# Modulation chunks of the first layer: three as rows on TensorE in the last head slots, one chunk step a head on VectorE, gate rows copied by ScalarE

## What is computed

```python
mod = (c_act @ ada_w[layer] + ada_b[layer])[:, None, :]
sh_a, sc_a, gt_a, sh_m, sc_m, gt_m = jnp.split(mod, 6, axis=-1)
h = modulate(rms_norm(x, attn_norm[layer]), sh_a, sc_a)
mix = diff_attention(h, a_w_in[i], a_w_out[i], a_lambda[i], a_subln[i], rel_bias, layer)
x = x + gt_a * mix
h = modulate(rms_norm(x, mlp_norm[layer]), sh_m, sc_m)
x = x + gt_m * squared_relu_mlp(h, mlp_w1[layer], mlp_w2[layer])
```

## Time and profile before

| what | us |
|---|---|
| median of 3 runs | 1377.74 |
| lowest, highest | 1368.96, 2510.94 |
| the profiled execution | 1370.68 |
| its span in the trace | 1368.9 |
| mean granted TensorE clock | 0.976 of 2.4 GHz |

### The profile page before, as it was taken

The page is one execution under the profiler, slowest core; times in us unless marked ns, Lnnn a source line. Parts: engine busy times, 40 slices in busy tenths (PEclk is TensorE's granted clock), DMA queues, the critical chain, the costliest instruction groups (busy, mean ns, idle before and its releaser), DMA issues.

```text
span 1368.9 us, 22008 instructions
## 1 busy us (share of the span) xinstructions
PE 1297.5 (95%) x8462; PEld 1125.1 (82%) x8462; DVE 883.9 (65%) x1593; ACT 682.8 (50%) x1196; POOL 139.0 (10%) x166
## 2 busy tenths in 40 slices
PE   7879899999989999989999988999999999999999
PEld 3678798998879865789999876799998777898987
DVE  3579789999676377785544676665655656644453
ACT  2546454435355346544545685554444566654442
POOL 0122111001000000010101121011010101011000
PEclk9989999999999799999999999999999999999999
DMA  9997449999787332286665252296565464466650
GB/s 350 344 290 230 159 136 341 331 332 332 250 246 197 119 124 94 64 289 208 183 192 166 91 184 63 93 272 225 178 189 171 138 194 140 134 194 186 186 166 32
DMA packets 144776, 267.42 MB, mean 195 GB/s; under 512 B 11040, under 2 KB 50208, under 8 KB 144288
## 3 DMA queue, kind: packets, MB, share of 16 engines
q1 hardware_dynamic: 138592, 250.94, 57.1%
q0 software_dynamic: 3456, 12.58, 2.8%
q10 hardware_dynamic: 2624, 2.49, 0.6%
HBM read 264.83 MB, written 1.15 MB: 194 GB/s over the span
## 4 chain that ended last, share of the span: by engine, by line
PE 67%; DVE 13%; DMA 7%; issue 6%; ACT 4%; SPq 1%; POOL 1%; DVEq 0%; ACTq 0%; POOLq 0%
PE bank L542 12%; PE bank L544 12%; PE bank L543 12%; DMA wring<-in_mlp_w 4%; PE ps_s L542 4%; PE ps_s L543 4%; PE ps_s L544 4%; PE ps_p L542 3%; PE ps_p L543 3%; PE ps_p L544 3%; DVE wlo L1585 3%; DVE acc L1604 3%; DMA xn<-in_ada_w 2%; ACT whi L2746 2%; DVE acc L1633 1%
## 5 line engine op out<-in xcount | busy, mean ns | idle before, releaser
L1585 DVE TENSOR_TENSOR wlo<-wring,whi 128x1024 fp32r<-128x1024 f32 (+1 forms) x376 | 455.0, 1220 | 298.4 <-ACT whi L2746 295.3
L2746 ACT ACTIVATE whi<-wring 128x1024 fp32r<-128x1024 f32 (+1 forms) x376 | 388.5, 1045 | 389.3 <-PE bank L544 143.2
L542 PE MATMUL bank<-h_hi,whi 128*128 128x256 f32 x1216 | 349.7, 288 | 5.6 <-DVE wlo L1585 3.2
L543 PE MATMUL bank<-h_lo,whi 128*128 128x256 f32 x1216 | 346.4, 285 | 0.0
L544 PE MATMUL bank<-h_hi,wlo 128*128 128x256 f32 x1216 | 346.2, 285 | 0.0
L542 PEld LDWEIGHTS bank<-h_hi,whi 128*128 128x128 f32 x1216 | 235.6, 194 | 11.0 <-issue 6.4
L543 PEld LDWEIGHTS bank<-h_lo,whi 128*128 128x128 f32 x1216 | 235.8, 194 | 0.7
L544 PEld LDWEIGHTS bank<-h_hi,wlo 128*128 128x128 f32 x1216 | 235.7, 194 | 0.0
L3405 POOL TENSOR_TENSOR ex<-ex 128x512 f32<-128x512 f32 x64 | 75.6, 1186 | 690.4 <-ACT g_hi L2877 690.4
L542 PE MATMUL ps_s<-whi,g_hi 128*128 128x512 f32 x256 | 101.9, 398 | 5.4 <-DVE g_lo L1854 5.2
L542 PE MATMUL bank<-whi,h_hi 128*128 128x512 f32 (+3 forms) x248 | 97.2, 392 | 8.9 <-DVE wlo L1585 3.2
(11 more groups left out here) (395 smaller groups left out, 1849.6 us busy)
## 6 DMA issues: line engine op xcount, KB each, us to landing
wring<-in_mlp_w SPq DMA_DIRECT2D x128, 512.0 KB, 4.5
wring<-in_ada_w SPq DMA_DIRECT2D x72, 512.0 KB, 7.5
wring<-in_mlp_w_in SPq DMA_DIRECT2D x64, 512.0 KB, 3.8
wring<-in_mlp_w_out SPq DMA_DIRECT2D x64, 512.0 KB, 4.2
wring<-in_a_w_in SPq DMA_DIRECT2D x24, 512.0 KB, 10.0
xn<-in_ada_w POOLq DMA_DIRECT2D x24, 512.0 KB, 4.7
wring<-in_moba_w_qkv SPq DMA_DIRECT2D x24, 512.0 KB, 4.3
wring<-in_kv_ada_w SPq DMA_DIRECT2D x16, 512.0 KB, 8.1
```

The lines of the kernel that those rows point to most:

```text
L542: nc.tensor.matmul(out, lh, rh, start=first, stop=False, skip_group_check=mixed)
L543: nc.tensor.matmul(out, lh, rl, start=False, stop=False, skip_group_check=mixed)
L1585: v.tensor_tensor(piece_view(wlo, p), raw_view(p), piece_view(whi, p).bitcast(F32), ALU.subtract).then_inc(lo_ready, 1)
L2746: a.activation(piece_view(whi, p), raw_view(p), ACT.Copy).then_inc(hi_ready, 1)
```

## The change

Chunks 9, 6 and 7 (`ROWS`) leave the matvec on VectorE. Their twelve loads go through the ring, four behind the pieces of each of the heads 5, 6 and 7, and TensorE runs `late_rows` on them behind the second product of slots 5, 6 and 7; ScalarE copies their banks into `acc`. Their column sums are made in `sum_columns`: chunk 9 at the end of slot 6, chunks 6, 7 and the last matvec chunk (8) together behind slot 7. VectorE has twelve chunk steps in place of twenty-four: four ahead of slot 0 as before, then one a slot, behind `diff_combine` in slots 0 to 2 and ahead of the second split from slot 3 on. GpSimd sends twelve chunk loads. The gate rows are copied by ScalarE in slot 7. The sum that stood between the last two parts of the `a_w_out` product is gone. The four chunks that used `late_rows` before are renumbered.

```diff
-MOD_SLOTS = (0, 2, 4, 6)
-CHUNKS = (4, 5, 8, 9, 6, 7)
+MOD_SLOTS = (0, 4)
+CHUNKS = (4, 5, 8)
+ROWS = (9, 6, 7)
...
     for h in range(8):
-        plan += a_qk(h)
+        plan += a_qk(h) + (ada(0, ROWS[h - 5:h - 4]) if h >= 5 else [])
...
+            def sum_columns(use, rows, chunks):
+
+                for i in rows:
+                    bank_emptied(pe, ("late_rows", i))
+                if chunks:
+                    pe.wait_ge(matvec_done, chunks)
+                sources = [i % 2 for i in rows] + ([2] if chunks else [])
+                b = bank_take(pe, use)
+                piece_of[use] = -1
+                for n, i in enumerate(sources):
+                    for j in range(4):
+                        last = nc.tensor.matmul(bank[:, b, 4 * n + j:4 * n + j + 1], acc[:, i, j * P:(j + 1) * P],
+                                                ones[:, 0:1], start=True, stop=True)
+                last.then_inc(filled[b], 1)
...
                 qk_piece(s, b, 1)
+                if s >= 5:
+                    late_rows(s - 5)
                 if s == 7:
                     gate_rows("a0", 16)
...
                 if s in MOD_SLOTS:
                     mod_columns(matvec_order[MOD_SLOTS.index(s)])
-
-            mod_columns(matvec_order[4])
+                if s == 6:
+                    sum_columns("rows_a", [0], 0)
+
+            sum_columns("rows_b", [1, 2], 3)
...
             diff_back(7)
-            pe.wait_ge(matvec_done, 6)
-            pe.wait_ge(sem("diff_evened"), 1)
-            for j in range(4):
-                last = nc.tensor.matmul(early_banks[0][:, j:j + 1], acc[:, 2, j * P:(j + 1) * P], ones[:, 0:1],
-                                        start=True, stop=True)
-            last.then_inc(sem("early_columns"), 1)
...
                 if slot_head(s - 3) is not None:
                     diff_even(slot_head(s - 3))
-                for i in range(2):
-                    chunk_step(4 + 2 * s + i)
-                    keep_ahead("dve", p + 1)
+                if s >= 3:
+                    chunk_step(4 + s)
+                keep_ahead("dve", p + 1)
                 if slot_head(s - 1) is not None:
                     diff_combine(slot_head(s - 1))
+                if s < 3:
+                    chunk_step(4 + s)
...
+                if s >= 5:
+                    late_sums(s - 5, acc[:, (s - 5) % 2, :])
+                if s == 7:
+                    for g in range(2):
+                        drain(("a0", "gate", g), gate_row[:, g * W:(g + 1) * W], (0, W))
...
-                if rstd_at[("diff", 0)] <= k < rstd_at[("diff", 6)]:
-                    n = 12 + 2 * (k - rstd_at[("diff", 0)])
-                    chunk_load(n)
-                    chunk_load(n + 1)
+                if rstd_at[("diff", 0)] <= k < rstd_at[("diff", 3)]:
+                    chunk_load(9 + k - rstd_at[("diff", 0)])
```

More of the change, by code:

```diff
@@ L428, in build @@
         matvec_order = [ada_order[c] for c in CHUNKS] + ada_order[10:22] + ada_order[26:28]
-        drain_order = [ada_order[c] for c in opening + CHUNKS] + ada_order[10:]
+        drain_order = [ada_order[c] for c in opening + CHUNKS[:2] + ROWS + CHUNKS[2:]] + ada_order[10:]
         def drained_by(*chunks):
@@ L435, in build @@
         chunk_buffers = [xn[:, i, :].rearrange("p (k n) -> p k n", n=W) for i in range(2)]
-        late = ada_order[22:26]
+        late = [ada_order[c] for c in ROWS] + ada_order[22:26]
         ROOT_EIGHTH = math.sqrt(0.125)
@@ L634, in gate_rows @@
                                                 ident[:, :], start=True, stop=True)
+                    if name == "a0":
+                        piece_of[name, "gate", g] = -1
                     last.then_inc(filled[b], 1)
@@ L735, in late_columns @@
             def late_columns(i):
-                bank_emptied(pe, ("late_rows", i))
+                bank_emptied(pe, ("late_rows", 3 + i))
                 b = bank_take(pe, ("late_mod", i))
@@ L1037, in _ @@
             mlp("m0", ada_order[10:22], lambda: gate_rows("m0", 40), inside=turn_inside)
-            late_rows(0)
-            late_rows(1)
+            late_rows(3)
+            late_rows(4)
             turn_scaled("kv", 1)
@@ L1229, in between @@
                 elif b < 8:
-                    late_rows(b // 2, 4 * (b % 2) + 2 * i, 4 * (b % 2) + 2 * i + 2)
+                    late_rows(3 + b // 2, 4 * (b % 2) + 2 * i, 4 * (b % 2) + 2 * i + 2)
                 elif b < 18:
@@ L1639, in chunk_step, with sum_drain @@
                     v.memset(stat[:, 1:2], 0.0).then_inc(matvec_done, 1)
[L1641 to L1647, removed]
+            def sum_drain(use, first, chunks):
+                src = bank_full(dve, use)
+                at, n = col["ada_b0"] + 4 * first, 4 * chunks
+                v.tensor_tensor(mod[:, 4 * first:4 * first + n], src[:, 0:n], params[:, at:at + n],
+                                ALU.add).then_inc(drained[uses[use][0]], 1)
+                bank_emptied(dve, use)
+                v.memset(stat[:, 1:2], 0.0).then_inc(mod_drained, chunks)
             def rstd(width, n, tag=None, eps=None):
@@ L2134, in _ @@
                     diff_even(slot_head(s - 3))
-                for i in range(2):
-                    chunk_step(4 + 2 * s + i)
-                    keep_ahead("dve", p + 1)
+                if s >= 3:
+                    chunk_step(4 + s)
+                keep_ahead("dve", p + 1)
                 if slot_head(s - 1) is not None:
                     diff_combine(slot_head(s - 1))
+                if s < 3:
+                    chunk_step(4 + s)
                 if slot_head(s - 3) is not None:
                     diff_low(slot_head(s - 3))
-                if s == 7:
-                    gate("a0")
             p = slot_piece(8)
             keep_ahead("dve", p)
-            mod_drain(matvec_order[4])
             diff_scores(7)
             diff_even(5)
-            chunk_step(20)
+            sum_drain("rows_b", ROWS[1], 3)
             keep_ahead("dve", p + 1)
@@ L2957, in _, with late_sums @@
             act.wait_ge(sem("subln_ready"), 1)
+            def late_sums(i, to):
+                key = ("late_rows", i)
+                a.activation(to, bank_full(act, key), ACT.Copy).then_inc(drained[uses[key][0]], 1)
             for s in range(8):
@@ L2987, in _ @@
             mlp("m0")
-            def late_sums(i):
-                key = ("late_rows", i)
-                a.activation(row_sums[i], bank_full(act, key), ACT.Copy).then_inc(drained[uses[key][0]], 1)
             last = last_of(("m0_w2", 7))
-            scaled_norm("kv", (hk_hi, hk_lo, gs2, mod[:, 48:56]), 4, 4096, last - 3, last, late_sums)
+            scaled_norm("kv", (hk_hi, hk_lo, gs2, mod[:, 48:56]), 4, 4096, last - 3, last,
+                        lambda t: late_sums(3 + t, row_sums[t]))
             for t in range(TT):
@@ L3075, in _ @@
                 if b in (5, 7):
[L3076 removed]
+                    late_sums(3 + (b - 1) // 2, row_sums[(b - 1) // 2])
                 if b == 6:
@@ L3411, in _ @@
                     pool.wait_ge(sem("a0_split"), 6)
-                    for n in range(12):
+                    for n in range(9):
                         chunk_load(n)
                 roots(k)
-                if rstd_at[("diff", 0)] <= k < rstd_at[("diff", 6)]:
-                    n = 12 + 2 * (k - rstd_at[("diff", 0)])
-                    chunk_load(n)
-                    chunk_load(n + 1)
+                if rstd_at[("diff", 0)] <= k < rstd_at[("diff", 3)]:
+                    chunk_load(9 + k - rstd_at[("diff", 0)])
             squares("m3")
```

8 lines of the change are left out of this document (3 added, 5 removed).

## The result

| | us |
|---|---|
| changed kernel, median of 13 runs | 1382.41 (1379.16 to 1384.32) |
| kernel before, median of 13 runs beside them | 1370.36 |
| ratio, 95% interval | 1.0088 (1.0074 to 1.0102) |
| the changed kernel's profiled execution, and its span | 1379.83, 1377.6 |

The changed kernel is slower by 0.9%, some 12 us. The interval excludes 1, so the slowdown is real, but it is under the 2% that the prediction took as the bound of a difference. The forecast was 1381. One of the 13 runs before is the one of 2510.94, which hardly moves a median. The page's head of the changed kernel answers to the earlier trace rows; the busy share fell from 95% to 94%.

The account below looks back on a forecast made before the run. TensorE, busy 95% of the span, was taken as the bound, so relieving VectorE pays only where TensorE waits. −15.5 + 5.5 + 16.0 + 4.2 = +10.2 on 1370.7 gives 1381, range 1362 to 1393.

Parts of the forecast that it names:

- The ring: Slots 5 and 6: TensorE waits 8.2 and 7.8 as weight pieces need ring slots late_rows must free; cost 16.0.
- The clock behind them: TensorE behind the two waits of slots 5 and 6: clock falls to half rate, 2.1 each, cost 4.2.
- late_rows: Slots 5 to 7: three calls on TensorE, 1.8 each, in the open; cost 5.5.
- The gap at 88.09: Head 0's turns: TensorE's wait of 7.79 for VectorE shrinks to about 1.3; gain 6.5.
- its clock: Behind the wait at head 0's turns: the 5.2 us at clock 0.50 go; gain 2.1.
- The small gaps: TensorE's later waits of 0.69, 0.93, 0.85 and 1.78 go, by fewer VectorE steps and ScalarE's gate-row copies; gain 4.25.
- the clock from 145.7: Stretch 145.7 to 151: the fall of the clock goes with the gaps of 0.85 and 1.78; gain 2.6.
- The sum: Whole kernel: gains of 15.5 against costs of 5.5, 16.0 and 4.2, net +10.2, so 1381.
- A: Slots 5 and 6: loads arrive in time, only late_rows is added; −10, 1361; chance 0.15.
- B: Front, slots 1 and 2: another load keeps the gap at head 0's turns; +19, 1390; chance 0.15.
- C: Slots 5 and 6: cheaper waits, no low clock, loads at the page's pace; +3, 1374; within the forecast's 0.70.

Follow-up runs that it names:

- experiment 1: Changed kernel with only the order of loads altered, so no early-split piece takes the ring slot of an unread chunk load: 1360.04, ratio 0.9941.
- experiment 2: Changed kernel with only chunk 7's four loads moved, behind the first two pieces of a_w_out: 1370.55, ratio 1.0007.
- experiment 3: Changed kernel with idle matmuls behind late_rows in slots 5 and 6: 1391.14 with 64 of them, 1376.31 with 32.
- experiment 8: The reordered kernel with the first half of each of the three new late_rows calls done twice: 1366.58, ratio 0.9978.
- experiment 4: Changed kernel run again unaltered, on another chip: 1383.09, ratio 1.0092.
- the reordered kernel: Changed kernel with chunk loads 9 and 6 behind heads 6 and 7, chunk 7 behind a_out's first two pieces: 1360.04; second run 1360.70.
- experiment 7: The reordered kernel with the gate rows copied by VectorE again, as before the change: 1360.53, ratio 0.9932.
- experiment 9: The reordered kernel with VectorE splitting pieces 9 to 12 ahead of the opening's last two chunk steps, no step in slot 0: 1356.09, ratio 0.9902.
- experiment 6: Changed kernel with its one chunk step ahead of the combine in slots 0 to 2 too: 1378.30, then 1381.87 when repeated.

## Why the prediction was right

**The ring (+16.0).** Right in place, kind and size: 7.90 + 7.57 = 15.5. The chain of slot 5 link by link, predicted and measured: 1.1 and 1.1 until SP sends, 5.0 and 4.2 for the transfer, 1.0 and 1.2 for ScalarE, 1.2 and 1.4 for VectorE's split (with a small drain that I had not counted), 1.1 and 1.1 for the scores, 0.7 and 0.8 for the evening. (My links add up to 10.1 and not 10.0, and the low end of my range, 1381 less 2.4 and 4, is 1375 and not 1373; neither matters.) The transfer was 0.8 shorter than my value. The Trainium skill (DMA: Bandwidth & Descriptors, Anatomy of one DMA) gave 3.2 as an estimate, for a load sent from GpSimd; the 4.2 of both slots, sent from SP, stands between that and the 5.0 and 4.6 that I took. Experiments 1 and 2 show that the order of the loads is the cause.

**The clock behind them (+4.2).** Right in kind, somewhat small: 4.8 to 5.5 by experiment 3. In the trace, against experiment 1, the stretch between the late gap and the next `late_rows` grew by 1.6 in slot 6 and 3.7 in slot 7, where the clock stayed down from 141.8 to 149, 5.3 together. The second is what I had too low.

**late_rows (+5.5).** Right: 1.92 a call, 1.85 until the next instruction starts, in the open by experiment 8.

**The gap at 88.09 (−6.5) and its clock (−2.1).** Right, and a little small: the signal came at 82.28 against my 81.3, and TensorE, held by its own wait near 66, came no sooner, so the whole 7.79 went. That it went whole is luck: in the executions in which TensorE's own wait was shorter a gap of up to 0.91 is left (experiment 4). The signal's time is no longer set by the chunk steps: VectorE waits 2.05 for ScalarE's split ahead of it. Between 81 and 106 the clock is at 1.00.

**The small gaps (−4.25) and the clock from 145.7 (−2.6).** They went, but two smaller ones came that I had not named: 0.41 at head 1's turns, and a wait that was 0.30 at 172.62 before is 1.08 now. The clock's share was right: `a_w_out` from its first matmul to its first wait took 10.59 before and 8.04 in the reordered kernel, 2.55 less. For the gate rows my reason was wrong: I gave the 1.78 to their move to ScalarE, and by experiment 7 it goes without that, by the lighter slot.

**The sum.** +10.2 predicted; +11.8 measured. Without the ring and its clock the prediction has −10.0, and experiment 1 measures −9.2. Its gains are larger by 1.3 (7.79 in place of 6.5), and what I had not named takes more than that back: 0.4 at head 1's turns, 0.8 for the part at 1.08, and 0.4 for the way to head 0's turns, which took 15.58 from piece 9 on in place of 15.20. There the clock was 0.85 against 0.89, behind a wait of 4.17 in place of 3.21; that wait is 2.9 to 4.5 in the executions of the changed and the reordered kernel, so this much is scatter. The remaining 0.5 I can't place.

**The rivals.** A (the loads are in time, 1361) is not what the changed kernel does, but it is what the reordered kernel does, 1360: its price was right. B (another load ends the gap at the front) didn't happen; ScalarE never waited for a load there. C (no fall of the clock) is refuted by the windows, though the transfer's part of it was half true.

## What to carry to other kernels

In a ring of buffers, find for each load whose slot it takes and when that reader is done: a load that takes the slot of something read in the same stage turns a prefetch into a round trip, here 8 us of wait each time, with 1.6 and 3.7 of clock behind it, and moving twelve loads by a few places in one queue was worth 21 us where the arithmetic moved between engines was worth 9. A step that waits for a transfer should not stand ahead of ready work on an engine that others wait for (experiment 9); where its load has landed its place is worth nothing (experiment 6). And a step put behind another is only put off; the gap goes for good when the engine has less to do.

## What was not expected of the hardware

The granted clock also fell while TensorE was busy. In the stretch with `a_w_out` it happened in some of the profiled executions and not in others, with the same instructions. Two windows of the reordered kernel's second run, with TensorE busy throughout, the first of them just behind the wait of 2.44 that ends at 149.84:

```profile
150.00:152.00 2.00, 2.00 (x8) 1.57 (x9) 1.55 (x3) 0.00 (x0) 0.00 (x0) 0.78 0.58 217
152.00:154.00 2.00, 2.00 (x6) 1.55 (x5) 0.00 (x0) 0.00 (x0) 0.00 (x0) 0.50 0.83 256
```

From there to the next wait it took 15.40 (149.84 to 165.24), and 13.79 in the first run of the same kernel (150.71 to 164.50). The same stretch took 13.79 in the changed kernel and 15.37 in its repeat. In experiment 7 the clock fell at about 140.5, behind the sums of the columns (24 matmuls of one column) and with no idle before it; from the last `late_rows` to the wait it took 19.29 against 17.72. Experiment 2 has two such falls. Each is worth 1.6, comes or stays away by itself, and goes into the stage's length: with them taken off, the stages of experiments 1 and 7 and of the repeat of 1 agree within 0.3 (108.8, 108.6, 108.8), and experiment 2 stands 9.8 under the changed kernel. What sets them off the runs don't show. The stretch ahead has a wait of 2.4 in the one case and instructions with few columns in the other, but the same wait and the same instructions also stand in executions in which the clock stayed at 1.00.
